# Rounded operands for the masks and logarithm sums of two attentions

## What is computed

```python
z = jnp.einsum('bhqd,bhkd->bhqk', q_blk, kh).astype(jnp.float32) * scale
mask = key_pos[None, :] < q_pos[:, None]
log_beta = jax.nn.log_sigmoid(z)
log_1m_beta = log_beta - z
l = jnp.where(mask, log_1m_beta, 0.0)
suffix = lax.cumsum(l, axis=3, reverse=True) - l
a = jnp.where(mask, jnp.exp(log_beta + suffix), 0.0)
```

```python
s = jnp.where(mask, s, -jnp.inf)
m = jnp.max(s, axis=-1, keepdims=True)
p = jnp.exp(s - m)
```

## Time and profile before

| what | value |
|---|---|
| median of 3 runs | 2649.77 us (2648.18 to 2650.36) |
| the profiled execution | 2649.93 us, its span 2648.1 us |
| busy over the span | PE 96%, DVE 76%, ACT 49%, POOL 10% |
| granted TensorE clock | 0.989 (1 is full speed) |
| DMA | 663.63 MB, mean 251 GB/s |
| chain that ended last | PE 75%, DVE 10%, DMA 5%, ACT 5% |
| largest group | WH<-RAW on ACT, 567 of 1059 ns |

### The profile page before, as it was taken

The page is one execution under the profiler, slowest core; times in us unless marked ns, Lnnn a source line. Parts: engine busy times, 40 slices in busy tenths (PEclk is TensorE's granted clock), DMA queues, the critical chain, the costliest instruction groups (busy, mean ns, idle before and its releaser), DMA issues.

```text
span 2648.1 us, 32249 instructions
## 1 busy us (share of the span) xinstructions
PE 2530.1 (96%) x12259; PEld 2106.3 (80%) x12259; DVE 2024.4 (76%) x2287; ACT 1297.5 (49%) x1652; POOL 264.0 (10%) x321
## 2 busy tenths in 40 slices
PE   5999899999999999999998999999899999999998
PEld 4777777777788888888876788887788888888887
DVE  6789858998887888798897788875766566665566
ACT  4544485434554445445435554456455544544453
POOL 0000120202020100202020000440000000020000
PEclk9999999999999999999999999999999999999999
DMA  8999849898888979897967766554556777766654
GB/s 312 314 335 330 272 164 322 320 333 279 274 315 293 339 278 339 268 359 255 334 219 241 248 193 197 147 164 139 192 178 229 226 231 226 225 220 191 191 188 146
DMA packets 298362, 663.63 MB, mean 251 GB/s; under 512 B 20752, under 2 KB 21104, under 8 KB 297184
## 3 DMA queue, kind: packets, MB, share of 16 engines
q1 hardware_dynamic: 294976, 650.21, 73.2%
q0 software_dynamic: 2656, 9.66, 1.0%
q10 hardware_dynamic: 576, 1.70, 0.2%
HBM read 659.39 MB, written 2.10 MB: 250 GB/s over the span
## 4 chain that ended last, share of the span: by engine, by line
PE 75%; DVE 10%; DMA 5%; ACT 5%; issue 4%; SPq 0%; DVEq 0%; POOL 0%; ACTq 0%
PE PS L607 75%; DVE WL L1394 3%; DVE ACC L1402 3%; ACT WH L1010 2%; DMA RAW<-in_w_in 2%; DVE UQ L1394 1%; DMA RAW<-in_w_o 1%; DMA RAWX<-in_w_a_up 1%; PE PS L610 1%; ACT L1010 1%; DMA RAWX<-in_w_ada 1%; DVE hn L1399 1%; DMA RAW<-in_w_ff 0%; ACT UQ L1010 0%; DVE acc L1394 0%
## 5 line engine op out<-in xcount | busy, mean ns | idle before, releaser
L1010 ACT ACTIVATE WH<-RAW 128x1024 fp32r<-128x1024 f32 x567 | 600.2, 1059 | 804.1 <-PE PS L607 609.1
L1394 DVE TENSOR_TENSOR WL<-RAW,WH 128x1024 fp32r<-128x1024 f32 x567 | 704.1, 1243 | 366.9 <-ACT WH L1010 364.9
L607 PE MATMUL PS<-WH,AH 128*128 128x512 f32 x2052 | 816.8, 398 | 27.8 <-DVE WL L1394 14.7
L607 PE MATMUL PS<-WH,AL 128*128 128x512 f32 x2052 | 803.3, 391 | 0.0
L607 PE MATMUL PS<-WL,AH 128*128 128x512 f32 x2052 | 803.0, 391 | 0.0
L607 PE MATMUL PS<-HL,WH 128*128 128x512 f32 x2048 | 729.6, 401 | 5.7 <-DVE HL L1394 5.7
L607 PE MATMUL PS<-HL,WL 128*128 128x256 f32 x2048 | 576.8, 282 | 0.0
L607 PEld LDWEIGHTS PS<-WH,AH 128*128 128x128 f32 x2052 | 388.0, 189 | 121.4 <-DVE WL L1394 29.9
L607 PEld LDWEIGHTS PS<-HL,WH 128*128 128x128 f32 x2048 | 386.8, 189 | 104.9 <-DVE HL L1394 9.1
L607 PEld LDWEIGHTS PS<-WH,AL 128*128 128x128 f32 x2052 | 387.3, 189 | 82.9
L607 PEld LDWEIGHTS PS<-WL,AH 128*128 128x128 f32 x2052 | 388.1, 189 | 77.8 <-issue 1.0
(11 more groups left out here) (237 smaller groups left out, 1962.5 us busy)
## 6 DMA issues: line engine op xcount, KB each, us to landing
RAW<-in_w_ff SPq DMA_DIRECT2D x335, 512.0 KB, 4.2
RAW<-in_w_ada SPq DMA_DIRECT2D x284, 512.0 KB, 5.0
RAW<-in_w_in SPq DMA_DIRECT2D x192, 512.0 KB, 4.6
RAWX<-in_w_ada SPq DMA_DIRECT2D x100, 512.0 KB, 5.4
RAWY<-in_w_ff SPq DMA_DIRECT2D x96, 512.0 KB, 4.1
RAWX<-in_w_ff SPq DMA_DIRECT2D x81, 512.0 KB, 5.1
RAWX<-in_w_in SPq DMA_DIRECT2D x48, 512.0 KB, 5.2
RAW<-in_w_out SPq DMA_DIRECT2D x32, 512.0 KB, 3.6
```

What stands on the lines that cost most here:

```text
L607: return e.matmul(o, l, r, start=start, stop=stop, skip_group_check=True)
L1010: return e.activation(o, i, f, **kw)
L1394: return e.tensor_tensor(o, a, b, op)
```

## The change

Both attentions get rounded (fp32r) operands for the matmuls that were f32 with constants.

First attention: `neglt`, `nge` and `nones` are cast once into STR and `ident` into IR (ACT, in stage 0 of head 0). DVE gets a stage 3, a tick after stage 2, that casts `e2` to E2H and subtracts to get E2L. PE's stage 4 becomes stage 5: two masks with IR, two sums with E2H and two with E2L. ACT's Exp into E3 moves from stage 4 to 5, and the last stage from 6 to 7 on PE, ACT and DVE. The lists of stages in `due` are (0, 2, 5, 7) on PE and ACT and (2, 3, 7) on DVE. DVE's stage 3 waits for PE's O of head h-2 (`s_stO`), which ACT's Exp waited for before.

Second attention: at j = DIL0 ACT casts the mask to CNR and `ident` to IR2, and PE's mask matmul uses them.

```diff
                         e.wait_ge(s_st3, h - 1)
                     mm(Z[:, 0:256], kt[:, 0:128], qt, True, False)
                     mm(Z[:, 256:384], kt[:, 128:256], qt[:, 128:256], False, True).then_inc(s_stZ, 1)
-                elif s == 4:
+                elif s == 5:
 
                     if h == 0:
-                        e.wait_ge(s_stat, 16)
-                    e.wait_ge(s_ste, 2 * h + 2)
-                    mm(Z[:, 0:128], ident, neglt, False, False)
-                    mm(Z[:, 256:384], ident, neglt, False, False)
-                    mm(Z[:, 0:384], nge, e2, False, False)
-                    mm(Z[:, 128:256], nones, e2[:, 256:384], False, True).then_inc(s_stE, 1)
-                elif s == 6:
+                        e.wait_ge(s_str, 1)
+                    e.wait_ge(s_sth, h + 1)
+                    high, low = E2H[:, h % 2, :], E2L[:, h % 2, :]
+                    neglt_r, nge_r, nones_r = [STR[:, 128 * i:128 * i + 128] for i in range(3)]
+                    mm(Z[:, 0:128], IR[:, :], neglt_r, False, False)
+                    mm(Z[:, 256:384], IR[:, :], neglt_r, False, False)
+                    mm(Z[:, 0:384], nge_r, high, False, False)
+                    mm(Z[:, 128:256], nones_r, high[:, 256:384], False, False)
+                    e.wait_ge(s_stl, h + 1)
+                    mm(Z[:, 0:384], nge_r, low, False, False)
+                    mm(Z[:, 128:256], nones_r, low[:, 256:384], False, True).then_inc(s_stE, 1)
+                elif s == 7:
                     e.wait_ge(s_st3, h + 1)
                     if h == 0:
                         eng, count = evac_of[bl.at["in1", 7]][1]
...
                     if h > 0:
                         e.wait_ge(s_dx, 2 * h)
                     else:
-                        e.wait_ge(s_cc, 32)
+                        e.wait_ge(s_ccr, 1)
                     mm(Z[:, 0:128], qk[:, 0:128], qk[:, 256:384], True, False)
                     mm(Z[:, 128:384], qk[:, 128:256], qk[:, 256:512], False, False)
-                    mm(Z[:, 0:384], ident, CCN[:, 384:768], False, True).then_inc(s_dZ, 1)
+                    mm(Z[:, 0:384], IR2[:, :], CNR[:, :], False, True).then_inc(s_dZ, 1)
                 elif s == 6:
                     e.wait_ge(s_dp, 4 * h + 1)
                     if h == 0:
...
                     e.wait_ge(s_stT, h + 1)
                     if h == 0:
                         e.wait_ge(s_vc, 4)
+
+                        e.wait_ge(s_stat, 16)
+                        af(STR[:, :], ST[:, 128:512], ACT.Copy)
+                        af(IR[:, :], ident, ACT.Copy).then_inc(s_str, 1)
                     if h > 1:
                         e.wait_ge(s_stE, h - 1)
                     af(qk[:, 0:256], PS[:, 4, 0:256], ACT.Copy, scale=SM[:, 0:1]).then_inc(s_stq, 1)
...
                 elif s == 2:
                     e.wait_ge(s_stZ, h + 1)
                     if h > 1:
-                        e.wait_ge(s_ste, 2 * h - 2)
+                        e.wait_ge(s_stE, h - 1)
                     af(e1, PS[:, 5 + b, 0:384], ACT.Abs).then_inc(s_stx, 1)
                     e.wait_ge(s_stx, 3 * h + 1)
                     af(e1, e1, ACT.Exp, scale=-1.0).then_inc(s_stx, 1)
                     e.wait_ge(s_stx, 3 * h + 2)
                     af(e1, e1, ACT.Ln, bias=1.0).then_inc(s_stx, 1)
-                elif s == 4:
+                elif s == 5:
                     e.wait_ge(s_stE, h + 1)
-                    if h > 1:
-                        e.wait_ge(s_stO, h - 1)
                     af(e3, PS[:, 5 + b, 0:384], ACT.Exp).then_inc(s_st3, 1)
-                elif s == 6:
+                elif s == 7:
                     e.wait_ge(s_stO, h + 1)
                     af(BH[:, 8 + h, :], PS[:, 7, 0:256], ACT.Copy).then_inc(s_bh, 1)
 
...
                     e.wait_ge(s_hm, 48)
                     e.dma_start(CCN[:, 0:384], C["cc"]).then_inc(s_cc, 16)
                     e.dma_start(CCN[:, 384:768], C["cn"]).then_inc(s_cc, 16)
+                if j == DIL0:
+                    e.wait_ge(s_cc, 32)
+                    af(CNR[:, :], CCN[:, 384:768], ACT.Copy)
+                    af(IR2[:, :], ident, ACT.Copy).then_inc(s_ccr, 1)
                 if j == ANG0 + 6:
                     e.wait_ge(s_an, 25)
                     af(sn, ang, ACT.Sin).then_inc(s_trig, 1)
...
                         e.wait_ge(s_msr, 8)
                         e.wait_ge(s_stat, 16)
                     if h > 1:
-                        e.wait_ge(s_stE, h - 1)
+                        e.wait_ge(s_sth, h - 1)
+                        e.wait_ge(s_stl, h - 1)
                     stt(e2, PS[:, 5 + b, 0:384], 0.0, e1, ALU.max, ALU.add).then_inc(s_ste, 1)
                     d = e2.rearrange("p (a t) -> p a t", t=128)[:, 0:3:2, :]
                     e.wait_ge(s_ste, 2 * h + 1)
                     tt(d, d, lt.unsqueeze(1).broadcast_to([128, 2, 128]), ALU.mult).then_inc(s_ste, 1)
-                elif s == 6:
+                elif s == 3:
+
+                    e.wait_ge(s_ste, 2 * h + 2)
+                    if h > 1:
+                        e.wait_ge(s_stO, h - 1)
+                    e.tensor_copy(E2H[:, b, :], e2).then_inc(s_sth, 1)
+                    e.wait_ge(s_sth, h + 1)
+                    tt(E2L[:, b, :], e2, f32(E2H[:, b, :]), ALU.subtract).then_inc(s_stl, 1)
+                elif s == 7:
                     e.wait_ge(s_bh, 8 + h + 1)
                     tt(BL[:, 8 + h, :], PS[:, 7, 0:256], f32(BH[:, 8 + h, :]), ALU.subtract).then_inc(s_bl, 1)
 
...
                             red(MS[:, n // 2 - 1, t, n % 2 * 4:n % 2 * 4 + 4], heads(TMP[:, t, :]), ALU.add).then_inc(s_msr, 1)
                 if QKN0 <= j < QKN0 + 4:
                     qk_norm((j - QKN0) // 2, (j - QKN0) % 2)
-                for h, s in due(p, STK0, 8, 2, (2, 6)):
+                for h, s in due(p, STK0, 8, 2, (2, 3, 7)):
                     stick(h, s)
                 n, r = divmod(p - MIX0, 4)
                 if 0 <= n < 4 and r < 2:
```

More of the change, by code:

```diff
@@ L402, in program @@
         phase.close()
+        phase = ExitStack()
+        sb("to_E1", [128, 2 * KT * S + 1024], F32, phase)
+        E2L = sb("E2L", [128, 2, 384], F32R, phase)
+        sb("to_E3", [128, 7 * 1024 - 768 + 2 * D + 2 * 512 + 512], F32, phase)
+        E2H = sb("E2H", [128, 2, 384], F32R, phase)
+        STR = sb("STR", [128, 384], F32R, phase)
+        IR = sb("IR", [128, 128], F32R, phase)
+        phase.close()
         def ff_memory(tag, stack):
@@ L438, in program @@
         CCN = sb("CCN", [128, 768], F32, phase)
+        CNR = sb("CNR", [128, 384], F32R, phase)
+        IR2 = sb("IR2", [128, 128], F32R, phase)
         phase.close()
@@ L446, in program @@
         E3 = SX[:, 512:1280].rearrange("p (b x) -> p b x", b=2)
-        lt, neglt, nge, nones = [ST[:, 128 * i:128 * i + 128] for i in range(4)]
+        lt = ST[:, 0:128]
         xT = XT0[:, :].rearrange("p (k s) -> p k s", s=S)
@@ L533, in program @@
             "turned", "qk", "z", "softplus", "masked", "e", "a", "o")]
+        s_str, s_sth, s_stl = sem("stick_constants"), sem("stick_hi"), sem("stick_lo")
         s_mg, s_mT, s_mh, s_ml = sem("merged"), sem("m_turned"), sem("m_hi"), sem("m_lo")
@@ L548, in program @@
         s_asq, s_att, s_aT, s_ath, s_atl = [sem("attn_" + x) for x in ("squares", "scaled", "turned", "hi", "lo")]
+        s_ccr = sem("cc_rounded")
         s_oag, s_rpn2 = sem("oa_gated"), sem("rope_products")
@@ L717, in stick @@
             def stick(h, s):
-                qk, e2, e3 = QKT[:, h % 2, :], E2[:, h % 2, :], E3[:, h % 2, :]
+                qk, e3 = QKT[:, h % 2, :], E3[:, h % 2, :]
                 T, Z, O = PS[:, 4, :], PS[:, 5 + h % 2, :], PS[:, 7, :]
@@ L919, in side @@
                     (pool_map if (p - POOL0) % 2 else pool_mix)((p - POOL0) // 2)
-                for h, s in due(p, STK0, 8, 2, (0, 2, 4, 6)):
+                for h, s in due(p, STK0, 8, 2, (0, 2, 5, 7)):
                     stick(h, s)
```

## The result

The change makes the kernel slower: 2659.48 us (2656.34 to 2663.85, eight runs) against 2651.40 (2647.68 to 2655.09, eight runs of the kernel before beside them). The ratio is 1.0033, with an interval of 1.0024 to 1.0041, which is 8.7 us (6.4 to 10.9). The forecast was 2647.3, 2.6 us faster, with a range of 2642 to 2653: both are missed, and the change went the other way. The profiled execution took 2659.18 us.

A forecast was written before the change was run, and what follows sets the result against it. The prediction took ACT to bound the first attention and PE the second. From the profiled 2649.93 us it took 3.4 for the second attention's mask and added 0.8 for the first attention: 2647.3 us, range 2642 to 2653.

The forecast's parts named there:

- What bounds the kernel: ACT is late in the first attention, PE's stalls on `e2` being its echo; PE bounds the second attention.
- Rival (a): First attention: PE is the bound after all, so its stalls and savings come off, giving 2636.4 us; chance 0.12.
- Part 1: Second attention, mask on PE: rounding saves 0.39 to 0.47 us a head, 3.1 to 3.8 in all, 3.4 taken.
- Part 2: First attention, PE's work: 0.6 us a head saved, 4.9 in all; only 1.5 us of ACT's waits for PE counted.
- Part 3: First attention, ACT's order: table loads go from 21 to 23; three more up to tick 105 cost 3.9 us.
- +0.8: First attention's net loss in the sum, the middle between 0 and +1.6 us reaching the stretch behind.
- Part 4: The rest: DVE's copy and subtraction, casts and new waits are hidden; the two DVE instructions unhidden would cost 1 us a head.
- (b): First attention: PE idles some 3 us twice waiting for ACT's copies and its clock halves, giving 2655.3 us; chance 0.06.
- Rival (c): First attention: one table load serves Exp and Ln, ACT loses some eight loads, giving 2636 us; chance 0.02.

The follow-up runs named there:

- sig_late: Kernel before, with the six Sigmoids of blocks 8 to 10 moved from ticks 94-107 to ticks 109-111: 2641.97 us, ratio 0.9969.
- rounded_old_ticks: Kernel before, with rounded operands in the first attention only, its stages kept in the old ticks: 2655.58 us, ratio 1.0014.
- sig_late_rounded_dil: Kernel before, with six Sigmoids moved to ticks 109-111, the second attention's mask rounded, and first-attention operands rounded in old ticks: 2638.67 us, ratio 0.9950.
- sig_late_changed: Changed kernel, with the six Sigmoids of blocks 8 to 10 moved to ticks 109-111: 2644.77 us, ratio 0.9970 to the kernel before.
- warm: Changed kernel, with 46 and 44 idle matmuls on PE ahead of its bank wait in heads 3 and 6: 2653.21 us, ratio 1.0015 to the kernel before.
- stick_only: Changed kernel with the second attention's rounded mask undone, so only the first attention changed: 2662.43 us, ratio 1.0041 to the kernel before.

## Why the prediction was wrong, by its own steps

**What bounds the kernel: right.** ACT was late in the first attention, and PE's stalls its echo; sig_late shows it. Rival (a) is refuted by rounded_old_ticks, though DVE's new work weighs on that kernel too, and by sig_late_rounded_dil: PE's saving shows only when the Sigmoids are gone.

**Part 1: right.** 3.1 to 3.8 us were forecast and 4.0 (1.3 to 6.6) measured; in the trace 0.46 us a head, eight times 3.7. The cast (1744.74, 0.52 us, and 0.30) was hidden.

**Part 2: the size nearly right, the conclusion wrong.** Six rounded matmuls take 0.82 us (371.09 to 371.91, the next weights), where I took 0.70. That PE's stalls would move from `e2` to ACT was right. That they would end on the copies of q and k, near 354 and 3 us long, was wrong: they end on `e3`, ahead of Z, at 364.84 and 399.56, 7.38 and 5.49 us long. The sum took ACT's waits for PE, 1.5 us in the rows before, as gone; they are 8.8 ahead of UQ alone.

**Part 3: the loads right, the step that failed.** 23 loads stand in the forecast ticks, and ACT's own work per tick is as counted: tick 95 is 5.55 us. What failed is the silent premise of the sum, that ACT waits for nothing but DVE's sums and PE for nothing but copies. I listed the waits that the change adds, and for `s_stO` I followed who waits. I didn't do so for two old waits on steps that are moved: `s_st3` ahead of Z, and `s_stE` ahead of the copies of q and k. Before, a tick lay between each and its releaser; the change used that up. The term "+0.8" should have held the loop. The cast at tick 106 was to begin 2.4 us later; counted from tick 91 it is 14.6. Of these, 6.1 remain with no Sigmoid in the way (sig_late_changed against sig_late). The other 8.5 are what the four Sigmoids cost more in the new order (13.5 between changed and sig_late_changed, 5.0 between before and sig_late): 3.4 of them go with the clock (warm), and the three more loads, 3.9 by my count, lie somewhere in the rest. No run prices the loads apart.

The Trainium skill (Perfetto Trace Analysis, "Matmuls") asks that independent matmul groups rotate through different PSUM banks, so that the reading of one overlaps the next's matmuls. This kernel does so with two banks, before and after, and PE waits 18.7 us in six places all the same. What the sentence doesn't say is when a bank must be free: two banks gave no overlap where the last reader came late in the very tick in which the next writer asked. By that rule alone the change would look harmless.

**Part 4: right as bounded, with an exception.** The copy and the subtraction take 0.35 and 0.56 us, 0.9 a head. In the old ticks they would have cost 0.8 a Sigmoid (rounded_old_ticks), near the 1 us that I gave for no cover. Beside POOL's all-reduce the copy costs more (below).

**The rivals.** (b), slower by the clock, named the point: idle stretches near 5 us. They came, and 2655.3 was its price. But it gave the whole loss to the clock, which is a quarter of it in the stretch and about half in the total. And I had the stalls at 3 us, because I counted only ACT's work and not the tick that PE waits for. The chance of 0.06 followed from that. Rival (c), one load for Exp and Ln together, is refuted again: every head has the loads apart.

**The range.** 0.80 for the forecast rested on the count of loads. A change that shifts stages of a loop between engines by a tick needs a rival in which a buffer is held longer; it had none.

## What to carry to other kernels

When a stage moves later, list all who wait for it, the old waits above all, with the tick at which each comes to its wait: buffers written in turn (here two PSUM banks) are the first place. Two engines that each wait for something the other makes in the same tick run in turn instead of together, and a wait on more than the last reader of a buffer (`s_stE` for `s_stZ`) can be one half of that: 7.6 us in one line where no Sigmoid stood in the way, 2.8 where they did. Work saved on an engine that isn't late is worth nothing (rounded_old_ticks), while six small Sigmoids taken from the engine that is late gave 8 us.

## What the runs showed of the hardware

**DVE beside POOL's all-reduce.** DVE's timeline of after, in the all-reduce (POOL, eight instructions, 344.44 to 360.08), and one cast out of it:

```profile
347.25 2.04 DVE L1418 TENSOR_TENSOR WL<-RAWX,WH 128x1024 fp32r<-128x1024 f32 x1 [0.57 <-ACT WH L1028]
349.22 1.25 DVE L1720 CAST E2H<-TMP 128x384 fp32r<-128x384 f32 x1
350.50 0.56 DVE L1418 TENSOR_TENSOR E2L<-TMP,E2H 128x384 fp32r<-128x384 f32 x1
350.97 2.13 DVE L1418 TENSOR_TENSOR WL<-RAW,WH 128x1024 fp32r<-128x1024 f32 x1
...
363.26 0.35 DVE L1720 CAST E2H<-TMP 128x384 fp32r<-128x384 f32 x1
```

The cast takes 1.25 us instead of 0.35, and WL 2.04 and 2.13 instead of 1.23. They stand on the chain to the Sigmoid that waits 2.48 us at 353.74. Others in the same stretch aren't slower (the subtraction, 0.56). It repeats: the cast takes 1.25 in stick_only and warm too, and in rounded_old_ticks, where it comes at another time, it takes 0.36 and the subtraction behind it 1.33. I had counted no price for neighbours. The Trainium skill (SBUF — State Buffer, "SBUF: two separate sides") has a port pair that DVE and GpSimd (POOL) share by an exclusive lock, not by splitting bandwidth: an instruction of DVE in a mode with two ports, or with two inputs in SBUF while GpSimd's instruction reads SBUF, waits until a GpSimd instruction that holds the pair has ended. Single delayed instructions beside undelayed ones agree with that; no run here shows which instruction held a lock.

**The same stall, two clocks.** Near 1830 us PE waits 2.82 us for DVE in both kernels, with the same work behind it. The windows that hold the stall's end (1824.49 and 1830.25), before and after:

```profile
1824.00:1830.00 6.00, 5.51 (x27) 4.61 (x28) 1.66 (x3) 2.32 (x5) 0.00 (x0) 1.00 0.27 87
```

```profile
1830.00:1836.00 6.00, 5.75 (x15) 4.64 (x16) 0.19 (x1) 0.17 (x1) 0.00 (x0) 0.50 0.26 87
```

It is 2.4 GHz once and 1.2 GHz the other time. So a few us of difference between two single traces can come from the clock. The whole times above come from five runs or more of each kernel; the stretches come from one trace each.
